# Moving four weight slots and their rounded copies by multiples of 64 bytes in a two-block fp32 layer kernel

## What is computed

```python
h = rms_norm(x, mix_norm)
... = split(h @ w_in)                       # mixers' inputs and 3 x 2048 gates
merged = sigmoid(g_a) * (y_a @ wb[:r_a]) + sigmoid(g_b) * (...) + sigmoid(g_c) * (...)
x = x + merged @ w_out
up = causal_dwconv(rms_norm(x, ffn_norm) @ w_up, conv_w, conv_b)
x = x + (silu(up[:, :5632]) * up[:, 5632:]) @ w_down
x = rms_norm(x, final_norm)
# second block, the same shapes: x @ w_in_2, two attentions, w_o_*, w_o_2, then
x = x + (silu(gt) * up) @ w_down_2
```

## Time and profile before

| what | value |
|---|---|
| median of 2 runs | 2951.97 us (2947.78 to 2956.16) |
| the profiled execution's own time | 2955.68 us |
| its span, first to last instruction | 2953.9 us |
| PE busy | 2915.8 us, 99% of the span |
| PEld (weight loads) busy | 2611.7 us, 88% |
| DVE busy | 2049.5 us, 69% |
| ACT busy | 1311.1 us, 44% |
| DMA | 531 MB, 51.3% of 16 engines' span |
| mean granted TensorE clock | 0.998 |

### The profile page before, as it was taken

How to read it: one execution, slowest core, us unless ns; L and a number is a source line. 1 busy time by engine, 2 the same in 40 slices (tenths; PEclk the granted TensorE clock), 3 DMA queues, 4 the chain that set the end, 5 groups by cost and what they waited for, 6 DMA issues and landing times.

```text
span 2953.9 us, 47041 instructions
## 1 busy us (share of the span) xinstructions
PE 2915.8 (99%) x18584; PEld 2611.7 (88%) x18584; DVE 2049.5 (69%) x2623; ACT 1311.1 (44%) x1418; POOL 69.9 (2%) x72
## 2 busy tenths in 40 slices
PE   8999999999999999999999999999999999999999
PEld 8898899999988888888888888877988888888888
DVE  6675798877788888885557777637666666665444
ACT  5354423444454444444444345426445444444333
POOL 0000000000001000000000000000000000000000
PEclk9999999999999999999999999999999999999999
DMA  6553334555555555555555555541555555555555
GB/s 233 185 185 134 116 115 157 167 177 190 195 188 196 192 192 196 189 180 186 187 189 202 192 185 177 181 148 72 186 197 187 196 192 191 196 189 180 192 195 185
DMA packets 87998, 531.06 MB, mean 180 GB/s; under 512 B 10080, under 2 KB 10976, under 8 KB 41824
## 3 DMA queue, kind: packets, MB, share of 16 engines
q1 hardware_dynamic: 87904, 529.76, 51.3%
HBM read 527.10 MB, written 2.10 MB: 179 GB/s over the span
## 4 chain that ended last, share of the span: by engine, by line
PE 96%; DVE 3%; ACT 1%; DMA 0%; issue 0%; SPq 0%; DVEq 0%; ACTq 0%
PE bank L594 74%; PE late L594 21%; DVE arena L1703 0%; DVE arena L1700 0%; DVE w_low L1703 0%; DVE half_low L1703 0%; ACT w_high L1219 0%; DVE arena L2005 0%; PE late L1160 0%; DMA ring<-in_w_gates 0%; DMA xT<-in_xT 0%; DVE small L2565 0%; ACT arena L1674 0%; DVE acts_both L1703 0%; DVE arena L2061 0%
## 5 line engine op out<-in xcount | busy, mean ns | idle before, releaser
L1703 DVE TENSOR_TENSOR w_low<-ring,w_high 128x2048 fp32r<-128x2048 f32 (+1 forms) x480 | 1014.2, 2113 | 386.4 <-ACT w_high L1219 382.5
L1219 ACT ACTIVATE w_high<-ring 128x2048 fp32r<-128x2048 f32 (+1 forms) x480 | 849.5, 1771 | 632.9 <-DMA ring<-in_w_down 225.9
L594 PE MATMUL bank<-up_early,w_high 128*128 128x512 f32 x1408 | 487.7, 389 | 0.0
L594 PE MATMUL bank<-up_late,w_high 128*128 128x512 f32 x1408 | 487.3, 389 | 0.0
L594 PE MATMUL late<-acts_both,w_high 128*128 128x512 f32 x1408 | 485.8, 392 | 0.3 <-DVE w_low L1703 0.3
L594 PE MATMUL late<-acts_both,w_low 128*128 128x256 f32 x1408 | 391.7, 278 | 0.0
L594 PE MATMUL bank<-up_late,w_low 128*128 128x256 f32 x1408 | 388.6, 276 | 0.0
L594 PE MATMUL bank<-up_early,w_low 128*128 128x256 f32 x1408 | 388.6, 276 | 0.0
L594 PEld LDWEIGHTS late<-acts_both,w_high 128*128 128x128 f32 x1408 | 264.5, 188 | 58.3 <-DVE w_low L1703 0.6
L594 PEld LDWEIGHTS bank<-up_early,w_high 128*128 128x128 f32 x1408 | 264.3, 188 | 55.1
L594 PEld LDWEIGHTS bank<-up_late,w_high 128*128 128x128 f32 x1408 | 264.3, 188 | 54.8
(11 more groups left out here) (312 smaller groups left out, 4885.0 us busy)
## 6 DMA issues: line engine op xcount, KB each, us to landing
ring<-in_w_up SPq DMA_DIRECT2D x176, 1024.0 KB, 4.7
ring<-in_w_down SPq DMA_DIRECT2D x128, 704.0 KB, 4.0
ring<-in_w_in SPq DMA_DIRECT2D x66, 1024.0 KB, 4.7
ring<-in_w_mix SPq DMA_DIRECT2D x62, 1024.0 KB, 4.8
ring<-in_w_gates SPq DMA_DIRECT2D x96, 512.0 KB, 3.7
ring<-in_w_branch SPq DMA_DIRECT2D x16, 1024.0 KB, 4.8
ring<-in_w_out SPq DMA_DIRECT2D x16, 1024.0 KB, 4.7
ring<-in_w_o SPq DMA_DIRECT2D x16, 1024.0 KB, 4.8
```

What stands on the lines that cost most here:

```text
L594: return nc.tensor.matmul(o, lhsT, rhs, start=first, stop=last)
L1219: A(w_high[:, s, 0:cols], ring[:, s, 0:cols], ACT.Copy).then_inc(rounded[s], 1)
L1703: return V.tensor_tensor(o, a, b, op)
```

## The change

The ring becomes one tensor of 4 x (2048 + 16) floats, of which each slot uses the first 2048: raw and lowered slots now begin 8256 bytes apart. The rounded slots become four tensors, slot s at 640 + 64 s bytes past its old multiple of 8192 in the arena (before: 960 for all). The half slots follow the ring's: `half_low` and `half_raw` in slots 0 and 1, `half_high` in slots 2 and 3. No instruction is added, removed or moved; operands' addresses alone change, and the tensors behind the ring start 256 bytes later.

Counted as above (modulo 256, from the ring's start; the 256 bytes drop out), the places go from `w_high` 192, `w_low` 0 in every slot to

| slot | w_high | w_low |
|---|---|---|
| 0 | 128 | 0 |
| 1 | 192 | 64 |
| 2 | 0 | 128 |
| 3 | 64 | 192 |

and those of the half slots from 0 and 0 to `half_high` 128, `half_low` 0 (half slots 0, 1) and 192, 64 (half slots 2, 3). The moving tiles stay at 0.

```diff
-W_SHIFT = 960
+LINE = 16
...
-        ring = sb("ring", [P, RING, UNIT])
-        ring_base = nc.sbuf_base - RING * UNIT * 4
+        slots = sb("ring", [P, RING * (UNIT + LINE)])
+        ring_base = nc.sbuf_base - RING * (UNIT + LINE) * 4
+        ring = slots.rearrange("p (s c) -> p s c", c=UNIT + LINE)[:, :, 0:UNIT]
...
-        w_low = alias("w_low", ring_base, [P, RING, UNIT])
-        w_high = alias("w_high", arena_base, [P, RING, UNIT], 94, W_SHIFT)
+        w_low = alias("w_low", ring_base, [P, RING, UNIT + LINE])[:, :, 0:UNIT]
+        w_highs = [alias(f"w_high{s}", arena_base, [P, UNIT], 94 + s * UNIT // T, 640 + 4 * LINE * s)
+                   for s in range(RING)]
...
-        half_raw = ring[:, 0:2].rearrange("p s (q c) -> p (s q) c", c=HALF)
-        half_low = alias("half_low", ring_base, [P, RING, HALF])
-        half_high = alias("half_high", ring_base, [P, RING, HALF], 2 * UNIT // T)
+        half_raws = [ring[:, s // 2, s % 2 * HALF:(s % 2 + 1) * HALF] for s in range(RING)]
+        half_lows = [w_low[:, s // 2, s % 2 * HALF:(s % 2 + 1) * HALF] for s in range(RING)]
+        half_highs = [w_low[:, 2 + s // 2, s % 2 * HALF:(s % 2 + 1) * HALF] for s in range(RING)]
...
-                mm(o, w_high[:, s, c], high, first, False)
+                mm(o, w_highs[s][:, c], high, first, False)
```

More of the change, by code:

```diff
@@ L508, in load_half @@
                         sp.wait_ge(consumed[q], units.consumed[q].value())
-                sp.dma_start(half_raw[:, s, 0:cols], src).then_inc(half_landed[s], 16)
+                sp.dma_start(half_raws[s][:, 0:cols], src).then_inc(half_landed[s], 16)
             def load_gate(c):
@@ L632, in mm3 @@
                 c = slice(c * P, (c + 1) * P)
-                mm(o, w_high[:, s, c], high, first, False)
-                mm(o, w_high[:, s, c], low, False, False)
+                mm(o, w_highs[s][:, c], high, first, False)
+                mm(o, w_highs[s][:, c], low, False, False)
                 return mm(o, w_low[:, s, c], high, False, last)
@@ L646, in body @@
                         c = slice(k * P, (k + 1) * P)
-                        mm(bank[s][:], w_high[:, s, c], pairs[k], k == 0, False)
+                        mm(bank[s][:], w_highs[s][:, c], pairs[k], k == 0, False)
                         last = mm(bank[s][:, 0], w_low[:, s, c], pairs[k][:, 0], False, k == KT - 1)
@@ L693, in tokens @@
                             k, c = 4 * q + j, slice(512 * j, 512 * (j + 1))
-                            mm(o, high[k][:, tok], w_high[:, s, c], k == 0, False)
+                            mm(o, high[k][:, tok], w_highs[s][:, c], k == 0, False)
                             mm(o, high[k][:, tok], w_low[:, s, c], False, False)
-                            last = mm(o, low[k][:, tok], w_high[:, s, c], False, k == KT - 1)
+                            last = mm(o, low[k][:, tok], w_highs[s][:, c], False, k == KT - 1)
                     last.then_inc(consumed[s], 1)
@@ L783, in down @@
                                 c = slice(k * P, (k + 1) * P)
-                                mm(bank[4 + b][:], w_high[:, s, c], acts_both[:, :, n], n == 0, False)
+                                mm(bank[4 + b][:], w_highs[s][:, c], acts_both[:, :, n], n == 0, False)
                                 last = mm(bank[4 + b][:, 1], w_low[:, s, c], acts_high[:, n], False, n == FF_TILES - 1)
@@ L839, in gate @@
                         k, c = KT // 2 * half + j, slice(j * P, (j + 1) * P)
-                        mm(bank[at][:, 0], half_high[:, s, c], h_high[:, k], k == 0, False)
-                        mm(bank[at][:, 0], half_high[:, s, c], h_low[:, k], False, False)
+                        mm(bank[at][:, 0], half_highs[s][:, c], h_high[:, k], k == 0, False)
+                        mm(bank[at][:, 0], half_highs[s][:, c], h_low[:, k], False, False)
                     pe.wait_ge(half_lowered[s], halves.lowered[s].value())
@@ L844, in gate @@
                         k, c = KT // 2 * half + j, slice(j * P, (j + 1) * P)
-                        last = mm(bank[at][:, 0], half_low[:, s, c], h_high[:, k], False, k == KT - 1)
+                        last = mm(bank[at][:, 0], half_lows[s][:, c], h_high[:, k], False, k == KT - 1)
                     last.then_inc(half_consumed[s], 1)
@@ L857, in _ @@
                             c = (2 * (h % 2) + n) * ML_DH + e
-                            last = mm(bank[4 + o // 2][q0:q1, o % 2], half_raw[:, s, c:c + q1 - q0], CA[:, k],
+                            last = mm(bank[4 + o // 2][q0:q1, o % 2], half_raws[s][:, c:c + q1 - q0], CA[:, k],
                                       n == 0, n == 1)
@@ L983, in _ @@
                     c = (f % 2 * S5_TILES + k) * P
-                    last = mm(bank[4 + f // 2][:, f % 2], half_raw[:, s, c:c + P], GA[:, k], k == 0, k == 3)
+                    last = mm(bank[4 + f // 2][:, f % 2], half_raws[s][:, c:c + P], GA[:, k], k == 0, k == 3)
                 if f % 2:
@@ L1218, in round_weights @@
                 act.wait_ge(landed[s], there)
-                A(w_high[:, s, 0:cols], ring[:, s, 0:cols], ACT.Copy).then_inc(rounded[s], 1)
+                A(w_highs[s][:, 0:cols], ring[:, s, 0:cols], ACT.Copy).then_inc(rounded[s], 1)
             def round_rounds(n, cols):
@@ L1403, in round_gate @@
                     act.wait_ge(half_landed[s], there)
-                    A(half_high[:, s], half_raw[:, s], ACT.Copy).then_inc(half_rounded[s], 1)
+                    A(half_highs[s], half_raws[s], ACT.Copy).then_inc(half_rounded[s], 1)
             act.wait_ge(conv_ready, 1)
@@ L1710, in lower_weights @@
                 dve.wait_ge(rounded[s], ahead.rounded[s].value())
-                tt(w_low[:, s, 0:cols], ring[:, s, 0:cols], w_high[:, s, 0:cols].bitcast(F32), SUB)\
+                tt(w_low[:, s, 0:cols], ring[:, s, 0:cols], w_highs[s][:, 0:cols].bitcast(F32), SUB)\
                     .then_inc(lowered[s], 1)
@@ L1935, in lower_gate @@
                     dve.wait_ge(half_rounded[s], half_units.rounded[s].value())
-                    tt(half_low[:, s], half_raw[:, s], half_high[:, s].bitcast(F32), SUB).then_inc(half_lowered[s], 1)
+                    tt(half_lows[s], half_raws[s], half_highs[s].bitcast(F32), SUB).then_inc(half_lowered[s], 1)
             dve.wait_ge(if_summed, 1)
```

## The result

The changed kernel takes 2991.23 us (median of two runs, 2991.12 and 2991.34) against 2951.97 before: a ratio of 1.0133, with a 95% interval of 1.0071 to 1.0195. By the 2% of the prediction that is "within 2%", and the time lies in the range that was given, 2920 to 2996. But it is 39 us above the predicted 2952 and outside the outcome that had the largest chance (mixed, 2938 to 2968, 0.45). It is within 3 us of rival B, in which all pairs are slow and which had 0.17; the range held because it took B in, 5 us from its upper end. So the class and the range held, while the main term of the sum did not. Ratios here leave out runs over 1.5% above the fastest of their kernel as slow, which happened to two of the ten runs of `st192` and to no other, while medians take all runs in.

What follows compares the result with a forecast made beforehand. PE's pace was taken as the bound, busy 99% of 2953.9 us. Gates -7.7, triples -3.8, tokens -1.0 and pairs +8.6 summed to -3.9 us on 2955.68, giving 2951.8, stated as 2952; range 2920 to 2996.

Steps and rivals of the forecast that it cites:

- mixed: Whole kernel: some pairs slow, some clean, with gains in gates, triples and tokens; 2938 to 2968 us, chance 0.45.
- rival B: Pairs lose their clean state and stay slow from the first `w_out` unit: +46.3 us, 2994 in all; chance 0.17.
- Rival D: The change costs DVE or ACT, 12 us in the gates: 2964 us; chance 0.04.
- Gates: 256-column gate matmuls: new places recover half of the 15.4 us lost against the clean pace, -7.7 us.
- Triples and tokens: Steps of three 256-column matmuls gain a third of 11.3 us, -3.8; 512-column token matmuls gain 1.0 us.
- Pairs: 512 + 256 column matmuls: a third of 5664 slow by 10 ns, 18.9 us less 10.3 already paid, +8.6.
- The prediction's own test: Up projections: all four slots at 5.44 us a unit means all clean; all at 5.6 means all pairs slow.
- Rival A: Addresses don't matter; pace depends on how loads fall in time after each PE stop: 2948 to 2956 us, chance 0.20.
- the rule: PE reads weights and moving data through two own ports, never waits, so every address term would be zero.
- The prediction's other rule: A warm 512-column matmul should take 215.8 ns; the trace's best is 226.7, so not borne out for fp32r.

Runs made afterwards that it cites:

- `st192`: Kernel before with raw and lowered slots moved by stage, at 64 for triples and gates, 0 for pairs, `w_high` kept at 192: 2954.94 us, ratio 1.0011.
- run 12: Kernel before with only the gates' half slots moved from place 0 to 64: 2938.75 us, ratio 0.9954.
- `oe`: Kernel before with slots at (w_high, w_low) places (64, 0), (64, 128), (192, 0), (192, 128): 2967.62 us, ratio 1.0040.
- Run 10: Kernel before with all four slots at (192, 64) from start to end: 2978.98 us, ratio 1.0097.
- runs 6 and 9: Kernel before, ring moved by stage (64 triples and gates, 0 pairs): `w_high` at 64 everywhere, 2987.51 us; `w_high` alternating 64 and 192, 2950.34 us.
- run 11: Kernel before with only the moving tile `up_late` 64 bytes further on: 2961.97 us, against 2949.15 before.
- `turn`: Kernel before with the four slots' `w_high` at 192, 448, 704 and 960, `w_low` at 0: 2948.69 us, beside 2948.74 for the kernel before.

## Why the prediction was right and wrong

**Bound and method: right.** PE's pace was the only thing that moved: PE's busy time took 34.7 of the 35.4 us, DVE's 2291 and ACT's 1912 ns stayed. Rival D had nothing to it.

**Gates: right in kind.** Predicted -7.7, measured -5.7 us. Of the 96 half units, 30 became clean (24 matmuls at 113.3 ns), all of them in half slots 2 and 3, at (192, 64); those with `half_high` at 128 over `half_low` at 0 go at 119 ns a matmul. With all at 64 (run 12) it is -8.3.

**Triples and tokens: right.** Predicted -3.8 and -1.0; measured -2.9 in `w_mix` and `w_mix2` and -1.3 in `w_branch`, and -1.7 for the tokens. Slot 2, named in the prediction as one as bad as the gates, has 5.72 us a unit, 119.2 ns a matmul. Slots 1 and 3 reached 113.3 and 113.8.

**Pairs: the step that failed.** It is "I take a third of the pairs slow: 18.9, less 10.3 now paid: +8.6". Measured: +48.5 us by the table of stages. Not a third but all 5664 pairs are slow, at a mean of 350.6 instead of the 350 that slow pairs had; (5664 - 1030) x 10.6 is 49. The size of a slow pair was right, the number of them was not. Two reasons stood behind the third. "It lies nearer to the clean end, since 4600 of 5664 are clean now" took the share of clean pairs at one place as the chance of any place; that cleanness belonged to (192, 0), and of the sixteen places only (64, 0) and (192, 0) have been seen clean. And "with four relations in turn, PE can't stay in one lucky state" took the slow pairs for a clean state lost in stepping. But in `oe` four places in turn come back to the clean pace in two slots each time, while in the changed kernel each slot has a steady pace in the up projections (346.8, 350.9, 353.3, 351.6) and none is clean. The prediction's own test decided it: "if all hold 5.6, B".

**Rival B: right in size, half right in cause.** It gave 2994 and all pairs slow from the first `w_out` unit, and so it was (the `w_out` units take 5.610 us, 350.6 ns a pair, from 748 us on). Its cause was a lost step that is never regained. Run 10 shows that no change of place is needed, and the changed kernel's slots keep their four paces turn after turn. A slow pace that stays does exist, at (64, 0) and (192, 0) (runs 6 and 9) and, in the first down of run 10, at (192, 64). In the changed kernel no sign of it was seen: its two runs agree within 0.2 us.

**Rival A and the rule.** By the Trainium skill ("SBUF — State Buffer", section "Who interferes with whom") PE reads through ports of its own and never waits for anyone; from this the prediction drew that no address matters. The runs do not bear that conclusion out: one moving tile 64 bytes on costs 6.4 us in each up projection (run 11), and (192, 64) instead of (192, 0) costs 9.3 (run 10). Whether PE waits there for another engine or for itself no run shows. What A saw is real, though: two paces at the same addresses.

The prediction's other rule is held against another case. The Trainium skill ("TensorE: Matmul & The Clock Gate", section "Back-to-back issue gap") gives columns / 2.4 + 2.5 ns for an isolated matmul. The 226.7 ns here are the pace of a stream with its weight loads, so they neither confirm nor refute it.

**What stays open.** Which of its paces (192, 0), (64, 0) or (192, 64) falls into. Something in how PE enters a stage may decide it, since the long stages keep their pace to the end, while in `w_in2` of the kernel before, where PE stops between groups of units, units change from 5.44 to 5.60 us and back, at units that hold a stop. That the 58 us between executions of `st192` come from this is likely, but one execution alone was profiled. The kernel before shows it too: its runs beside the experiments lie between 2947.3 and 2957.4, and the 7 us between a first down of 3.740 us a unit and one of 3.850 (64 units) would explain that; `turn`, the same kernel by its places, was profiled at 2948.69 with a clean first down, the kernel before at 2955.68 with a slow one. Nor is it shown what inside the chip collides, only that weights' and moving tiles' places decide it. A version with the gates' half slots at 64 and `w_mix2` alone moved to odd places (16 units x 0.21 = 3.4 us more, by `st192` against before) was not tried.

## What to carry to other kernels

In this kernel, where PE is busy for 99% of the time with a weight load for each 256 to 512 columns of fp32r, the addresses of weights modulo 256 bytes, relative to the moving tile's, are worth up to 4% of a pair's time (340 to 353 ns) and up to 6% of a 256-column matmul's (113 to 120 ns). In another such kernel compute each place before moving anything, treat the good place of each pattern (here (192, 0) for pairs, odd and odd for triples and gates, though `w_mix` was slow at (192, 64)) as a property to be kept, and move only the tiles whose pattern gains; a shift of the ring that all patterns share gave 13 us and took 49. When one set of addresses has shown two paces in a trace, its share of clean stages says nothing of another place: measure new places before counting on them. Judge by several runs, since one run of such a kernel can be off by tens of microseconds, and look whether the runs fall into groups before comparing medians.

## What the runs showed that was not expected

- The same pace in the up projections whether all slots lie at (192, 64) or one in four does: 5.547 and 5.548 us a unit. A full table of sixteen, reaching from 5.44 to 5.653 us, in which 256 bytes are a whole number of turns.
- The patterns differ: (192, 64) is clean for the triples of `w_mix2` (5.440) and slow for pairs (5.547).
- A pair has several paces at the same addresses: 340 and 350 ns at (192, 0), 340, 350 and 353.3 at (64, 0), 346.6 and 353.4 at (192, 64), kept over up to 88 units. The first down at (192, 0) was slow in one execution (before) and clean in another (`turn`). `st192`, whose long pair stages were all clean when profiled, is the least steady kernel: 58 us over ten runs, against 0.2 over the two of the changed one.
- DVE and ACT show none of it: 2291 ns and 1912 to 1914 ns for 2048 floats in the kernels before, after, `oe` and `upmove`.
